# Channel sums of a recurrent mixer's banded products: one float32 product against two products of split halves

## The reference, cut to what matters

```python
def step(S, inp):
    qc, kc, vc, gc = inp                       # one chunk of 64 tokens
    G = jnp.cumsum(gc, axis=2)
    o = jnp.einsum('nhtk,nhkv->nhtv', qc * jnp.exp(G), S)
    decay = jnp.exp(jnp.where(causal, G[:, :, :, None] - G[:, :, None], NEG))
    A = jnp.einsum('nhtk,nhsk,nhtsk->nhts', qc, kc, decay)
    o = o + jnp.einsum('nhts,nhsv->nhtv', A, vc)
```

## Time and profile before

| | |
|---|---|
| three runs | 2951.99, 2956.65, 2960.41 us |
| profiled execution: its time | 2955.95 us |
| profiled execution: its span, first to last instruction | 2954.0 us |
| mean granted TensorE clock | 0.988 of full speed |
| PE busy | 2867.6 us, 97% of the span |
| VectorE, ScalarE, GpSimd busy | 37%, 22%, 35% |
| VectorE busy from 104.4 to 138.9 us, the stretch of the banded products of head 0 | 28.92 of 34.50 us |

### The profile page before, as it was taken

How to read it: one execution, slowest core, us unless ns; L and a number is a source line. 1 busy time by engine, 2 the same in 40 slices (tenths; PEclk the granted TensorE clock), 3 DMA queues, 4 the chain that set the end, 5 groups by cost and what they waited for, 6 DMA issues and landing times.

```text
span 2954.0 us, 56225 instructions
## 1 busy us (share of the span) xinstructions
PE 2867.6 (97%) x21017; PEld 2664.9 (90%) x21017; DVE 1086.6 (37%) x2298; ACT 640.9 (22%) x1441; POOL 1036.7 (35%) x1060
## 2 busy tenths in 40 slices
PE   7999999999999999999998999999999999999999
PEld 5898998888999999999887787878789999999999
DVE  4767777321020010111436666666650110101103
ACT  5121221223101101001444333332351001000014
POOL 4000000445333334334754333333274334334344
PEclk8999999999999999999999999999999999999999
DMA  7311111554324311111233424343431111111112
GB/s 259 101 44 45 37 45 37 162 160 121 96 75 128 96 47 50 38 54 39 61 105 92 149 93 144 103 134 109 128 114 50 38 50 47 45 50 41 52 42 80
DMA packets 314743, 247.99 MB, mean 84 GB/s; under 512 B 19651, under 2 KB 299062, under 8 KB 313158
## 3 DMA queue, kind: packets, MB, share of 16 engines
q1 hardware_dynamic: 296578, 219.45, 24.1%
q10 hardware_dynamic: 9796, 17.81, 1.7%
q0 software_dynamic: 8192, 8.40, 1.1%
HBM read 222.87 MB, written 22.74 MB: 83 GB/s over the span
## 4 chain that ended last, share of the span: by engine, by line
PE 92%; DVE 2%; ACT 2%; POOL 1%; DMA 1%; issue 1%; SPq 1%; POOLq 0%; DVEq 0%; ACTq 0%
PE bank L2340 24%; PE bank L2342 23%; PE bank L2341 23%; PE bank L2826 2%; PE bank L2945 2%; PE bank L2847 2%; PE bank L2459 1%; POOL hl L777 1%; PE bank L2608 1%; PE bank L2868 1%; PE bank L2580 1%; PE bank L2933 1%; PE bank L2625 1%; DMA adae<-in_w_ada 1%; PE bank L2815 1%
## 5 line engine op out<-in xcount | busy, mean ns | idle before, releaser
L2340 PE MATMUL bank<-hh,whi 128*128 128x344 f32 (+1 forms) x3468 | 1141.0, 329 | 41.5 <-POOL hl L777 14.5
L2341 PE MATMUL bank<-hl,whi 128*128 128x344 f32 (+1 forms) x3468 | 1115.4, 322 | 0.0
L2342 PE MATMUL bank<-hh,wlo 128*128 128x344 f32 (+1 forms) x3468 | 1114.7, 321 | 0.0
L2340 PEld LDWEIGHTS bank<-hh,whi 128*128 128x128 f32 x3468 | 657.2, 190 | 82.8 <-issue 33.0
L2341 PEld LDWEIGHTS bank<-hl,whi 128*128 128x128 f32 x3468 | 657.2, 190 | 2.4 <-issue 1.0
L2342 PEld LDWEIGHTS bank<-hh,wlo 128*128 128x128 f32 x3468 | 657.1, 189 | 0.6
L746 POOL CAST whi<-wst 128x1024 fp32r<-128x1024 f32 (+4 forms) x222 | 180.6, 813 | 1008.2 <-PE bank L2342 726.6
L1915 DVE TENSOR_TENSOR atmp<-sil,bank 128x344 f32<-128x344 f32 x132 | 67.6, 512 | 940.1 <-PE bank L2342 926.0
L748 POOL TENSOR_TENSOR wlo<-wst,whi 128x1024 fp32r<-128x1024 f32 (+4 forms) x222 | 400.9, 1806 | 17.8
L2340 PE MATMUL bank<-ahi,whi 128*128 128x344 f32 x1056 | 338.7, 321 | 0.0
L2341 PE MATMUL bank<-alo,whi 128*128 128x344 f32 x1056 | 337.4, 320 | 0.0
(11 more groups left out here) (360 smaller groups left out, 3140.3 us busy)
## 6 DMA issues: line engine op xcount, KB each, us to landing
wst<-in_w_gu SPq DMA_DIRECT2D x88, 512.0 KB
adaw<-in_w_ada SPq DMA_DIRECT2D x40, 1024.0 KB, 5.4
pk<-in_cache_ckv SPq DMA_DIRECT2D x256, 128.0 KB, 2.5
wst<-in_w_in_even SPq DMA_DIRECT2D x28, 512.0 KB
wst<-in_w_down SPq DMA_DIRECT2D x32, 384.0 KB
wst<-in_w_down SPq DMA_DIRECT2D x32, 320.0 KB
adae<-in_w_ada SPq DMA_DIRECT2D x4, 2048.0 KB, 15.9
pr<-in_cache_krope POOLq DMA_DIRECT2D x256, 32.0 KB, 2.3
```

Source lines behind the costliest of these rows:

```text
L2340: mm(out, wh_, xh_, start=start, stop=False)
L2341: mm(out, wh_, xl_, start=False, stop=False)
L2342: return mm(out, wl_, xh_, start=False, stop=stop)
```

## The change

Each `ed` piece gets a high half (ScalarE copies it into a float32r tile `ed_hi`, which rounds it) and a low half (GpSimd subtracts the high half from `ed`, in place, as float32r). PE then multiplies a float32r matrix of ones with the two halves, accumulated in the bank, in place of one float32 product. New are two semaphores, 48 copies on ScalarE, 48 subtractions on GpSimd, one copy of the ones, and a phase `mixer` in GpSimd's queue. `ones_r` and `ed_hi` lie in slots 3 and 7 of `xT`, so ScalarE waits for `x_saved` earlier than before, in head 0 ahead of the first copy. The copies stand in ScalarE's queue between those for the banks and for the weights; the high halves of the later weights come behind them.

```diff
+        ones_r = spilled(HEADS - 1, "ones_r", [P, P], R)
+        ed_hi = [nc.alloc_sbuf_tensor_at(f"ed_hi{b}", [P, 512], R, offset=w_at - (2 * KT + 1) * N * 4 + b * 2048) for b in range(2)]
+        ed_lo = [nc.alloc_sbuf_tensor_at(f"ed_lo{b}", [P, 512], R, offset=ed_at[b]) for b in range(2)]
...
# GpSimd
+            def mixer():
+                for h in range(HEADS):
+                    for n, (d, _, nb) in enumerate(PIECES):
+                        w = nb * (BL - d)
+                        pool.wait_ge(ed_high, 12 * h + n + 1)
+                        nc.gpsimd.tensor_tensor(ed_lo[n % 2][:, 0:w], ed[n % 2][:, 0:w], ed_hi[n % 2][:, 0:w].bitcast(F),
+                                                ALU.subtract).then_inc(ed_low, 1)
...
-            phases = [setup, out_proj, lambda: ffn(0, G_FFN0, HI_FFN0, 2), latents, pairs,
+            phases = [setup, mixer, out_proj, lambda: ffn(0, G_FFN0, HI_FFN0, 2), latents, pairs,
...
# ScalarE
+                    def product_high(n):
+                        d, _, nb = PIECES[n]
+                        w = nb * (BL - d)
+                        act.wait_ge(e_ready, 12 * h + n + 1)
+                        nc.scalar.copy(ed_hi[n % 2][:, 0:w], ed[n % 2][:, 0:w]).then_inc(ed_high, 1)
...
+                    if h == 0:
+                        act.wait_ge(x_saved, 16)
+                        nc.scalar.copy(ones_r[:], ones[:])
+                    product_high(0)
+                    product_high(1)
                     split_high(s + 4)
                     for c in range(NC):
                         filled(SLOT_CG, c)
                         nc.scalar.copy(ug[:, 2 + c * CW:2 + (c + 1) * CW], bank[c][:, 0:CW]).then_inc(bank_free[c], 1)
                         if c < 2:
                             tokens(c, vtok[:, 4 * c:4 * c + 4, :])
+                        product_high(2 * c + 2)
+                        product_high(2 * c + 3)
                     split_high(s + 5)
+                    for n in range(8, 12):
+                        product_high(n)
                     split_high(s + 6)
...
# PE
                     pe.wait_ge(bc_free[n % 2], BC[n % 2] * h + n // 2 + 1)
-                    pe.wait_ge(e_ready, 12 * h + n + 1)
-                    mm(bank[6 + n % 2][:, 0:w], ones[:], ed[n % 2][:, 0:w], start=True, stop=True).then_inc(bc_ready[n % 2], 1)
+                    pe.wait_ge(ed_low, 12 * h + n + 1)
+                    mm(bank[6 + n % 2][:, 0:w], ones_r[:], ed_hi[n % 2][:, 0:w], start=True, stop=False)
+                    mm(bank[6 + n % 2][:, 0:w], ones_r[:], ed_lo[n % 2][:, 0:w], start=False, stop=True).then_inc(bc_ready[n % 2], 1)
```

More of the change, by code:

```diff
@@ L287, in trunk @@
         mq = lay("mix", "mq", [P, T])
+        ed_at = [at0 + used["mix"] + b * 2048 for b in range(2)]
         ed = [lay("mix", f"ed{b}", [P, 512]) for b in range(2)]
@@ L474, in trunk @@
         act_ready, ahi_ready, alo_ready = map(sem, ("act_ready", "ahi_ready", "alo_ready"))
+        ed_high, ed_low = sem("ed_high"), sem("ed_low")
         qk_hi, rope_sum = sem("qk_hi"), sem("rope_sum")
```

## The result

The changed kernel takes 2963.17 us (median of 10 runs, 2958.81 to 2966.45); the kernel before, on the same chip, 2954.69 us (10 runs, 2951.99 to 2960.41). The ratio is 1.0026, with a 95% interval of 1.0018 to 1.0034: 8.5 us slower. The profiled execution took 2962.27 us, with a span of 2960.3 us.

A forecast was written before the change was run, and what follows sets the result against it. PE was taken as the bound, VectorE close behind and, once delayed, setting each head's end: 2955.95 us + 6.6 for four longer heads + 3 for half clock = 2965.5, stated as 2965 us; range 2942 to 2977 us.

The forecast's parts named there:

- within: Whole kernel: outcome no more than 0.3% from the kernel before, either way; chance 0.38.
- slower: Whole kernel: outcome more than 0.3% slower than the kernel before; chance 0.42.
- PE's work: Broadcast products of each head: float32r takes 4.14 us instead of 7.74, giving PE 3.6 us per head, 14.4 in all.
- ScalarE, `x_saved`, the first two pieces: Mixer: ScalarE's copies, its earlier wait for the DMA, and pieces 0 and 1 would cost nothing.
- VectorE's delay: Mixer: GpSimd's low-half subtractions hold up VectorE's two-SBUF-operand work by 5.9 us per head, bounds 0 and 9.62.
- my list: Banded products: VectorE lines with two SBUF operands, L1720, L1722, L1739, L1698, L1498, open to hold-up by GpSimd.
- third rival: Mixer: GpSimd shuts VectorE out for its full durations, 9.6 us per head, giving 2980 us; chance 0.15.
- The end of a head: Head 0: attend(7) ends at 140.5 us, not 138.88; each head 1.65 us longer, four heads 6.6 us.
- Each head's broadcasts 1.7 us later than the last head's: Sign in the new profile: against before, each head's broadcasts start 1.7 us later than the previous head's.
- Clock: Mixer: new PE idle time beside attend brings half-clock stretches costing 3 us for four heads, bounds 0 and 6.
- The first: Rival: VectorE isn't held up in the mixer, attend(7) ends 3.4 us earlier per head, 2942 us; chance 0.17.
- The second: Rival: about half the VectorE delay, 3 to 4.5 us per head, 2951 to 2957 us; chance 0.18.

The follow-up runs named there:

- e1: Changed kernel without GpSimd's 48 subtractions, PE multiplying the high half twice and leaving the low half out; 2941.20 us, ratio 0.9954 to the kernel before.
- e3: Changed kernel with two scratch memsets on GpSimd in place of each subtraction, low half left out; 2944.84 us, ratio 0.9966 to the kernel before.
- e2: Changed kernel with GpSimd subtracting a constant tile into scratch, nobody waiting for it, low half left out; 2957.84 us, ratio 1.0012 to the kernel before.
- e7: Changed kernel with only pieces 0 to 5 split, the others kept as float32 products; 2947.96 us, ratio 0.9973 to the kernel before.
- e8: Changed kernel with VectorE making all low halves itself and GpSimd idle in the mixer; 2958.86 us, ratio 1.0009 to the kernel before.

## Why the prediction was right

The forecast was 2965 us, 9 us slower; it is 2963.17 us, 8.5 us above the kernel before. The difference, 0.26% by the ratio, lies just inside the bound of 0.3% on which the forecast's middle stood. So the outcome fell under "within", which had been given 0.38, and not under "slower", which had 0.42; yet the interval (1.0018 to 1.0034) does tell it from no difference. By its steps:

**PE's work: right.** 0.23 us a product of 512 columns, two per piece; e1, with a stretch 3.1 us shorter, shows that PE can use most of it.

**ScalarE, `x_saved`, the first two pieces: right.** PE waits for no copy of a product in the changed kernel. In ScalarE's timeline the copy of `hv` starts at 99.58 us, `ones_r` at 99.92 us and the pieces at 100.12 us; nothing waits for the DMA.

**VectorE's delay: right, piece by piece.** 34.03 us less 28.2 us of work are 5.8 us per head; the forecast was 5.9. The timelines of head 0, before and after, give for each piece how much longer the VectorE operation took that ran into its low half (us):

| piece | 2 | 3 | 4 | 5 | 6 | 7 | 8 | 9 | 10 | 11 | sum |
|---|---|---|---|---|---|---|---|---|---|---|---|
| forecast | 0.24 | 0.84 | 0.71 | 0.71 | 0.57 | 0.57 | 0.98 | 0.71 | 0.43 | 0.16 | 5.92 |
| measured | 0.26 | 0.96 | 0.71 | 0.68 | 0.57 | 0.57 | 0.96 | 0.66 | 0.48 | 0.23 | 6.08 |
| line held up | L1728 | L1730 | L1752 | L1728 | L1752 | L1728 | L1750 | L1728 | L1769 | L1769 | |

The groups by shape in the changed kernel show the same over all heads:

```profile
L1730 DVE COPY ki<-k 128x128 f32<-128x128 f32 x30 | 10.4, 347 | 0.1
...
L1752 DVE TENSOR_TENSOR ed<-mq,hk 128x384 f32<-128x384 f32 x12 | 9.5, 794 | 0.4
...
L1750 DVE TENSOR_TENSOR mq<-mq,hf 128x384 f32<-128x384 f32 x4 | 6.1, 1526 | 0.1
...
L1767 DVE TENSOR_TENSOR dtmp<-bank,hv 128x384 f32<-128x384 f32 x12 | 6.6, 548 | 0.0
```

```profile
L814 POOL TENSOR_TENSOR ed_lo<-ed,ed_hi 128x384 fp32r<-128x384 f32 x12 | 16.1, 1344 | 24.4 <-ACT ed_hi L1149 24.4
...
L814 POOL TENSOR_TENSOR ed_lo<-ed,ed_hi 128x512 fp32r<-128x512 f32 x12 | 15.6, 1315 | 284.7 <-ACT ed_hi L1149 284.7
```

The multiply out of a bank is spared, as was said: 548 ns at 384 columns, 549 before. The operations with two SBUF operands are stretched (the 384-column product 558 ns before, 794 now; mq of 384 columns 558 and 1526). But the copy into `ki`, with one SBUF input, wasn't on my list and took up to 1.18 us for its 0.22. And GpSimd's 384-column operation became 0.33 us longer than in the earlier trace rows, where I had said 0.2. The copy changes no sum, since the delay just lands on whatever VectorE runs next. Nor does GpSimd's greater length: part of it is GpSimd's own waiting. Its subtraction of 114.81 us is issued 0.06 us after VectorE's add of 114.75 us, which ends at 115.38 us, and ends 0.89 us after that; alone it takes 1.02 us.

The Trainium skill ("SBUF — State Buffer", "Who interferes with whom") has the second instruction fully blocked when VectorE's has two SBUF inputs and GpSimd's reads SBUF. The trace agrees on the victims it names, on the banks' multiply and, by e3, on GpSimd's writes. It also agrees that the later one is blocked until the other is done, in either direction: a held VectorE operation ends 0.41 us after GpSimd's, and the subtraction of 114.81 us does its work behind the add. What the trace doesn't bear out is my third rival, which made the price GpSimd's whole busy time. GpSimd is busy 11.96 us in the window of head 0, and VectorE loses 5.8 us: of each subtraction's length, GpSimd's own waiting costs VectorE nothing, and the held operation saves some 0.15 us of its own (0.41 us behind GpSimd's end, and not 0.56).

**The end of a head: right.** Forecast: attend(7) ends at 140.5 us, 1.65 us later against the broadcasts. It ends at 140.12 + 1.11 = 141.23 us, and everything before this mixer was 0.66 us later already (first broadcast at 105.09 for 104.43 us), which I can't put down to the change. So the head is 1.7 us longer. The waits stand where they were foretold, at broadcast 5, 9 and attend(7), and were 0.99 + 2.02 + 0.99 = 4.0 us; by the sum (3.6 us of work less, 1.7 us more in all) PE stood idle 5.3 us, so 1.3 us of it have no name in that view. Some of that is the way a wait is counted, from the end of the last record, which is longer than what its matmul costs (a product of 128 columns: a record of 0.27 us, a cost of about 0.06).

*Each head's broadcasts 1.7 us later than the last head's* did not show so evenly: the first 896-column multiplies of the four heads start 0.3, 5.1, 5.6 and 7.7 us behind those of the kernel before. The stretches of heads 0 to 2 are 1.7, 1.7 and 2.2 us longer and that of head 3, with half-clock time in it, 3.5 us; the rest of these steps fits the half-clock time between the stretches, of which the changed kernel has 6.8 us between heads 0 and 1 and the kernel before 3.4 us between heads 1 and 2.

**Clock: right in place, and in size by what was hidden, with a part given back.** Windows of 5 us of the changed kernel, the first two behind attend(7) of head 0, the third behind broadcast 9 of head 2, the last two from broadcast 9 to attend(7) of head 3 (the columns of the earlier trace rows); the kernel before has PEclk 1.00 in each of these windows, and its own low ones in the earlier trace rows:

```profile
140.00:145.00 5.00, 4.54 (x48) 4.48 (x49) 4.79 (x10) 0.00 (x0) 0.00 (x0) 0.78 0.02 3
145.00:150.00 5.00, 5.00 (x31) 4.98 (x30) 4.74 (x7) 0.59 (x1) 0.00 (x0) 0.87 0.36 105
370.00:375.00 5.00, 5.00 (x45) 4.98 (x43) 4.79 (x10) 0.70 (x2) 1.18 (x2) 0.66 0.02 3
485.00:490.00 5.00, 2.93 (x36) 2.31 (x36) 4.83 (x10) 0.92 (x2) 1.39 (x2) 0.76 0.01 3
490.00:495.00 5.00, 5.00 (x20) 5.00 (x21) 4.69 (x8) 0.30 (x1) 0.95 (x2) 0.56 0.00 0
```

These windows hold the 1.2 GHz stretches: PE had waited for GpSimd or VectorE just before, and attend's matmuls of 8 columns are among its work. Over the mixer PE ran at half clock for 34.1 us where it was 23.9, 5.1 us of work lost where I had taken 3, with bounds of 0 and 6. Not all of it counts: the stretches of heads 2 and 3 hold 10.2 us of half clock, which is 5.1 us of PE's work, and are together only 2.3 us longer than two of head 0, since PE waits less where it is slower. The prediction had named this hiding, but put no figure to it. At the mixer's end (the reciprocal of the last head starts at 545.80 us, before at 535.85 us) the changed kernel is 9.95 us behind, 9.3 without the late start; the forecast was 9.6. By its two parts that is 6.8 us for four heads and 2.5 us that the clock really cost. By the end of the span it is 6.3 us behind. Of the 3.6 us given back, the clock record accounts for 1.8 (20.9 us at half clock after the mixer, 24.5 before); the rest stays open. So the median's nearness to 2965 us leans on time given back outside the mixer, which nobody forecast, as well as on the right mechanism.

**The rivals.** The first, no hold-up, is what e1 does (2941.20 us for the 2942 it was priced at), but the changed kernel doesn't. The second asked for 3 to 4.5 us of delay; e2 has 4.2 us, the changed kernel 5.8. The third asked for 9.6.

**Slips in the sums.** The 0.7 us to the median was taken off where it should have been added (the profiled execution lies below the median), which would make 2966 us. The 0.14 us of overlap and 0.14 us of saved length behind the 0.31 us per piece make 0.28. The third rival's 144.2 less 138.88 is 5.3 us and not 5.4. None of them changes what was forecast by more than 1.5 us.

## What to carry to other kernels

Before an operation is moved to an engine that is idle, ask what its operands' memory does to the engine beside it: here ten GpSimd subtractions per head, 9.6 us if left alone, cost VectorE 5.8 us, more than the 4.3 us that VectorE needed to do the operation itself. An engine at 84% of a stretch in which another is the bound has little to give: VectorE had 3 us of waiting per head and was held up for 5.8, so that PE's 3.6 us could not be used. Split such a change by its pieces and keep those that fall into the waits of the engine that suffers. By the traces four of the twelve pieces were best (1.40 us per head, against 0.71 for two and 0.78 for six); the times of the three don't differ, and all lie some 6 us above e1's, in which nothing held VectorE up.

## What the runs showed of the hardware

A VectorE copy of 128 x 128 from SBUF to SBUF, with one input, was held up by GpSimd's subtraction: 1.18 us for 0.22. The Trainium skill names copies among the operations that can contend with GpSimd ("SBUF — State Buffer", "Who interferes with whom"); the trace agrees, and I had left this one out. Memsets on GpSimd, busy 7.95 us in head 0, held it up hardly at all (e3: that copy 230 ns in the mean and 291 at most, for 221). A GpSimd subtraction of the same size took 1102 ns when both inputs were one constant tile (e2) and 1344 ns on the real operands; this was not followed further. A VectorE operation with two SBUF inputs that ran into a GpSimd subtraction ended 0.41 us after it, at 384 columns (the changed kernel, at 116.27 and 130.00 us). The time at half clock moved with small shifts of the waits, from 13.7 us of the mixer (e7) to 37.5 us (e8), and so moved the kernel by several us beyond what the edits themselves account for.
